# The conditioning product of a two-block transformer kernel: two of its three groups leave block 1

## The chip, the cores and the metric

The kernel runs on one core of a Trainium2 chip. Its time is the device time of one execution in microseconds (us). Three runs of the kernel before gave 1567.90, 1569.79 and 1571.73 us, median 1569.79. TensorE, the matrix engine, is called PE here, VectorE DVE, ScalarE ACT and GpSimd POOL; SP is the engine whose queue issues the loads. [...]

## The reference: what is computed

256 tokens of width 1024 pass through two transformer blocks, all in float32.

Block 1: RMS norm, input projection, a pooling mixer and an attention of 8 heads, output projection with a residual, then a mixture of 32 experts (4 per token), and a final RMS norm. Block 2: a norm, an input projection into 3342 columns, 16 heads of three kinds of attention (6 with a decay, 4 of mLSTM kind, 6 of block kind), an output projection and a gated feed-forward. Block 2 is conditioned on a vector `c`:

```
mod = silu(c) @ w_ada + b_ada                  # 1024 x 6144 weights, 24 MB
sh1, sc1, g1, sh2, sc2, g2 = split(mod, 6)
hn = rms(x, norm1_g) * (1 + sc1) + sh1         # first norm of block 2
x  = x + g1 * (mixer(hn) @ w_out)
hn = rms(x, norm2_g) * (1 + sc2) + sh2         # second norm
x  = x + g2 * ((silu(gate) * up) @ w_down)
```

The product with `w_ada` depends on `c` alone and can be done at any time before its first use. Group 0 of its columns is sh1 and sc1 (used by the first norm of block 2), group 1 is g1 and sh2, group 2 is sc2 and g2 (used only after the attention of block 2).

## The kernel before, in words

All weights come through one ring of 12 slots of 1 MB in SBUF. SP walks a fixed list of chunks (`load(n)`, then a loop over the experts) and, for chunk n, waits until chunk n - 12 has been used (`chunk_used`, counted up by PE). So the order in which PE uses chunks is the order of the list, and a chunk that is moved in PE's program is moved in the list too. An expert takes 12 chunks: 8 of gate and up weights, 4 of down weights.

The conditioning product is 24 chunks, 8 per group. One chunk is `ada(i)` (line 528): four matmuls of 128x512 into the four column strips of PSUM bank 7. A group's eighth chunk is followed by `keep_ada(g)` on DVE (bank 7 plus bias into `mod`), by `turn_mod(g, b)` on PE (four transposes into bank b, line 738) and by `keep_mod(g, b)` on DVE (the turned columns into `modc`). Before: chunks 0 and 1 run at the start, 2 and 3 after the input projection, 4 and 5 ahead of the attention of block 1, 6 to 17 between its heads, 18 to 23 after the output projection.

`attention(block, extra)` is written as a pipeline over heads. In its step i PE does the scores of head i (lines 644 to 649), then what `extra` has for i, then the transposes of the probabilities of head i - 1 (line 670), then the product with the values of head i - 2 (lines 678 to 680). Between the scores and the transposes of a head stand a row maximum on DVE and the exponentials on ACT. Every engine runs its program in order.

After the attention of block 1: two chunks of the output projection on the pooled half (`project_out_start`, line 695) stand beside a chain of norms on DVE that ends in `att_rows`; then transposes of those rows (line 727), the other 6 of 8 parts of the projection, the norm of the rows, their transposes (`turn_rows(4)`), the router, and the loop over the experts. After the experts: sums, the final norm on DVE and ACT, `turn_rows(6)` on PE, and the input projection of block 2 (`project`, line 545).

## Time and profile before

| | |
|---|---|
| runs, median (us) | 1569.79 |
| profiled execution, span from first to last instruction (us) | 1568.5 |
| mean granted PE clock | 0.971 |
| PE busy | 1475.2 us, 94% of the span |
| DVE busy | 324.1 us, 21% |
| ACT busy | 221.4 us, 14% |
| bytes moved, mean rate | 496.98 MB, 317 GB/s |
| chain that ended last | PE 59%, DMA 20%, SP's queue 15%, DVE 3%, issue 2%, ACT 1% |

The profiled execution's span is 1.3 us below the median of the runs. A share of busy time is an average over stages: block 1 ahead of the experts fills about 155 us, the experts 950 us, block 2 460 us. PE's busy time counts occupied time at either clock, so it does not tell a slow stretch from a fast one; PEclk does.

### The profile page before, as it was taken

Reading aid. Unit: us, or ns where it says so; the run is one execution under the profiler, and the core shown is the slowest. Engines: PE = TensorE matmul, PEld = TensorE weight load, DVE = VectorE, ACT = ScalarE, POOL = GpSimd, SP = SyncE. Lnnn points to the kernel's source line nnn. Section 1 sums busy time; section 2 is a strip of 40 time slices with the busy share of each in tenths; the row PEclk is TensorE's granted clock in tenths of the full one; section 3 lists DMA queues with packets and bytes.
Section 4 is the critical chain, followed back from the end, with each engine's and each line's share of the span. In section 5 each row is a group of like instructions: output and inputs, shape, how many; then the busy total and the mean of one; then the engine's idle time right before and its main releaser. Section 6 shows DMA issues by size and latency. Waiting matters only on the chain.

```text
span 1568.5 us, 18813 instructions
## 1 busy us (share of the span) xinstructions
PE 1475.2 (94%) x7278; PEld 787.3 (50%) x7278; DVE 324.1 (21%) x861; ACT 221.4 (14%) x405; POOL 21.8 (1%) x14
## 2 busy tenths in 40 slices
PE   7999999999999999999999999999699998999998
PEld 5655443343343343343333334334499664888843
DVE  5535321121111121121111111112312533000001
ACT  1321011011111011011011111101212430000100
POOL 3100000000000000000000000000000000000000
PEclk9998999999999999999999999999799968999999
DMA  9996999999999999999999999999944103444400
GB/s 331 351 407 264 357 419 417 416 419 419 415 418 419 416 418 418 418 417 418 419 416 419 418 416 418 419 417 414 295 156 156 54 1 107 135 152 143 134 0 27
DMA packets 127123, 496.98 MB, mean 317 GB/s; under 512 B 9825, under 2 KB 51506, under 8 KB 91026
## 3 DMA queue, kind: packets, MB, share of 16 engines
q1 hardware_dynamic: 126484, 495.47, 79.9%
q10 hardware_dynamic: 606, 1.06, 0.2%
q8 instruction: 22, 0.36, 0.1%
q14 instruction: 11, 0.09, 0.0%
HBM read 495.44 MB, written 1.05 MB: 317 GB/s over the span
## 4 chain that ended last, share of the span: by engine, by line
PE 59%; DMA 20%; SPq 15%; DVE 3%; issue 2%; ACT 1%; DVEq 0%; ACTq 0%
DMA ring<-in_w_gate_up_dram 19%; PE PS L989 10%; SPq L459 9%; PE PS L803 9%; PE PS L545 8%; PE PS L828 8%; SPq L462 5%; PE PS L789 5%; PE PS L1005 5%; PE PS L695 3%; PE PS L836 3%; PE PS L644 2%; PE PS L528 1%; ACT work L1155 1%; PE PS L670 1%
## 5 line engine op out<-in xcount | busy, mean ns | idle before, releaser
L803 PE MATMUL PS<-ring,work 128*64 128x512 f32 x2048 | 461.4, 597 | 25.5 <-DMA ring<-in_w_gate_up_dram 25.5
L803 PEld LDWEIGHTS PS<-ring,work 128*64 128x64 f32 x2048 | 138.0, 137 | 331.1 <-issue 232.2
L828 PE MATMUL PS<-ring,work 128*64 128x512 f32 x1024 | 225.1, 592 | 0.0
L1624 DVE TENSOR_SCALAR work<-PS 128x512 f32<-128x512 f32 x32 | 22.1, 691 | 679.9 <-PE PS L803 679.9
L989 PE MATMUL PS<-ring,cols 128*128 128x256 f32 x704 | 156.0, 383 | 2.1 <-issue 2.1
L989 PEld LDWEIGHTS PS<-ring,cols 128*128 128x128 f32 x704 | 134.7, 192 | 20.8 <-DVE cols L1331 2.5
L828 PEld LDWEIGHTS PS<-ring,work 128*64 128x64 f32 x1024 | 71.7, 137 | 132.0 <-issue 129.6
L545 PE MATMUL PS<-ring,cols 128*128 128x240 f32 (+3 forms) x576 | 121.8, 374 | 4.1 <-DVE cols L1331 2.1
L789 PE MATMUL PS<-work,rows 128*128 128x64 f32 x1056 | 125.0, 278 | 0.0
L789 PEld LDWEIGHTS PS<-work,rows 128*128 128x128 f32 x1056 | 123.8, 196 | 0.8 <-DVE work L1601 0.8
L545 PEld LDWEIGHTS PS<-ring,cols 128*128 128x128 f32 x576 | 110.4, 196 | 13.4 <-DVE cols L1331 2.5
L1152 ACT ACTIVATE work<-work 128x512 f32<-128x512 f32 x32 | 20.1, 630 | 469.2 <-DVE work L1624 469.2
L1005 PE MATMUL PS<-ring,work 128*128 128x512 f32 x176 | 75.8, 593 | 0.7 <-ACT work L1282 0.7
L836 PE MATMUL PS<-work 64*128 64x512 f32 x264 | 65.6, 615 | 0.7 <-ACT work L1158 0.7
L695 PE MATMUL PS<-ring,cols 128*128 128x512 f32 x128 | 55.6, 593 | 0.8 <-DVE cols L1333 0.8
L1005 PEld LDWEIGHTS PS<-ring,work 128*128 128x128 f32 x176 | 33.4, 190 | 42.6 <-issue 41.6
L1158 ACT COPY work<-PS 128x512 f32<-128x512 f32 x32 | 18.7, 585 | 236.1 <-PE PS L828 236.1
L836 PEld LDWEIGHTS PS<-work 64*128 64x128 f32 x264 | 22.7, 186 | 43.1 <-issue 41.5
L1619 DVE TENSOR_TENSOR work<-PS,vcol 128x512 f32<-128x512 f32 x33 | 22.8, 691 | 99.2 <-PE PS L789 99.2
L1152 ACT ACT_TABLE_LOAD x32 | 41.1, 1283 | 0.6
L695 PEld LDWEIGHTS PS<-ring,cols 128*128 128x128 f32 x128 | 24.1, 190 | 30.8 <-issue 29.2
L1829 DVE TENSOR_TENSOR rows<-work,PS 128x512 f32<-128x512 f32 x11 | 7.6, 688 | 152.8 <-PE PS L989 152.8
(261 smaller groups left out, 859.6 us busy)
## 6 DMA issues: line engine op xcount, KB each, us to landing
ring<-in_w_gate_up_dram SPq DMA_DIRECT2D x278, 1024.0 KB, 20.4
ring<-in_w_down_dram SPq DMA_DIRECT2D x139, 1024.0 KB, 22.2
ring<-in_w_ada_dram SPq DMA_DIRECT2D x24, 1024.0 KB, 15.9
ring<-in_w_in_dram SPq DMA_DIRECT2D x13, 960.0 KB, 10.8
ring<-in_w_out_dram SPq DMA_DIRECT2D x8, 1024.0 KB, 10.9
ring<-in_w_in_dram SPq DMA_DIRECT2D x3, 1024.0 KB, 12.8
x_sb<-in_x_dram SPq DMA_DIRECT2D x2, 512.0 KB, 3.8
work<-in_band_dram SPq DMA_DIRECT2D x1, 1024.0 KB, 14.9
```

The source lines that it names most:

```text
L459: sp.dma_start(ring[:, s, :], gu_dram[bass.ds(e * KD + c, 1), :, :] .rearrange("o p n -> (o p) n")).then_inc(landed[s], 16)
L462: sp.dma_start(ring[:, s, :].rearrange("p (o k n) -> p o k n", o=1, k=2), dn_dram[bass.ds(e * 4 + (c - KD), 1), :, :, :] .rearrange("o p k ...
L545: mm = pe.matmul(bank(b)[:, t * w:(t + 1) * w], cols[:, k, t * P:(t + 1) * P], chunk(n)[:, k, :], start=(k == 0), stop=(k == KD - 1))
L644: pe.matmul(s[:, a:a + w], q[:, t * P:(t + 1) * P], k[:, 0:w], start=True, stop=ml)
L695: mm = pe.matmul(bank(2 * t + h), cols[:, k, t * P:(t + 1) * P], chunk(base_n + c)[:, k % 2, h * 512:(h + 1) * 512], start=(k == 0), stop= ...
L789: mm = pe.matmul(bank(2)[:, k * CAP:(k + 1) * CAP], rows[:, t, k * P:(k + 1) * P], sel_g[:, t, :], start=(t == 0), stop=(t == NT - 1))
L803: mm = pe.matmul(bank(b)[CAP * h:CAP * (h + 1), :], xg[:, k, :], w[:, b * FE + h * 512:b * FE + (h + 1) * 512], start=False, stop=(k == KD ...
L828: mm = pe.matmul(bank(3)[CAP * h:CAP * (h + 1), :], lhs, w[:, (f % 2) * D + h * 512:(f % 2) * D + (h + 1) * 512], start=False, stop=(f == 7))
L836: mm = pe.matmul(bank(4 + 2 * t + h), sel_t[CAP * h:CAP * (h + 1), t * P:(t + 1) * P], yb[CAP * h:CAP * (h + 1), :], start=False, stop=False)
L989: mm = pe.matmul(bank(4 + 2 * (j % 2) + up)[:, t * CW:(t + 1) * CW], cols[:, k, t * P:(t + 1) * P], chunk(n)[:, k, :], start=(k == 0), sto ...
L1005: mm = pe.matmul(bank(4 + 2 * t + h), h_t[:, f, t * P:(t + 1) * P], chunk(N_DN2 + f // 2)[:, f % 2, h * 512:(h + 1) * 512], start=(f == 0) ...
L1152: return nc.scalar.activation(sg, g_min, ACT.Sigmoid, scale=ALPHA).then_inc(done, 1)
```

## The change

The list of chunks, PE's program and DVE's program are rewritten so that only chunks 0 to 7 (group 0) are computed in block 1: 0 to 3 where they were, 4 to 7 after the output projection. Group 1 (chunks 8 to 15) runs after the experts, once DVE has read the sums from PSUM (`x_summed`), ahead of `turn_rows(6)`; it is turned after two chunks of block 2's input projection. Group 2 (chunks 16 to 23) runs in the second attention, two chunks after the scores of each of the heads 11 to 14 of 16, and is turned in the middle of the second output projection. The gains of the second norm are computed there too. A few small loads come earlier in the list.

```diff
+N_OUT1 = N_KVB + 1
+N_ADA0 = N_OUT1 + 4
+N_MOE = N_ADA0 + KD - ADA_NEXT
+N_ADA1 = N_MOE + EXPERTS * SLOTS
+N_IN2 = N_ADA1 + KD
+N_ADA2 = N_IN2 + len(IN2_CHUNKS)
+N_OUT2 = N_ADA2 + KD
...
             pe.transpose(bank(6)[:, 0:NVEC], vec[:, :], ident[0:NVEC, 0:NVEC]).then_inc(sig["vec2_turned"], 1)
-            ada(ADA_NEXT)
-            ada(ADA_NEXT + 1)
...
-            attention(1, {0: adas(6, 8), 1: adas(8, 9), 2: [pool_sums] + adas(9, 10), 3: adas(10, 12), 4: adas(12, 14),
-                          5: adas(14, 16), 6: adas(16, 17), 7: adas(17, ADA_MID)})
+            attention(1, {2: [pool_sums]})
...
-            for i in range(ADA_MID, ADA_MID + 3):
+            for i in (ADA_NEXT, ADA_NEXT + 1):
                 ada(i)
-            turn_mod(0, 6)
-            turn_mod(1, 5)
-            ada(ADA_MID + 3)
...
             turn_rows(4)
-            ada(ADA_MID + 4)
+            ada(ADA_NEXT + 2)
...
-            ada(ADA_MID + 5)
+            ada(ADA_NEXT + 3)
...
+            pe.wait_ge(sig["x_summed"], 2)
+            for i in range(KD, 2 * KD):
+                ada(i)
             turn_rows(6)
...
-            between = {}
+            between = {2: [lambda: turn_mod(1, 7)]}
...
-            attention(2, started=2)
+            attention(2, {i: adas(2 * KD + 2 * (i - ML_HI - 1), 2 * KD + 2 * (i - ML_HI)) for i in range(ML_HI + 1, ML_HI + 5)},
+                      started=2)
...
             project_out_start(N_OUT2)
+            turn_mod(2, 4)
             project_out_end(N_OUT2)
...
-            attention(1, {0: [lambda: keep_ada(0), square_pooled], 1: [keep_pooled], 3: [keep_pool_sums],
-                          5: [lambda: keep_ada(1)]})
+            attention(1, {0: [square_pooled], 1: [keep_pooled], 3: [keep_pool_sums]})
...
-            keep_mod(0, 6)
-            keep_mod(1, 5)
             keep_cols(lambda k: col("g_ffn_norm", k))
...
             do.step(v.memset(conv_x[:, :, 0:3], 0.0))
+            keep_ada(1)
+            keep_mod(1, 7)
...
+                          ML_HI + 5: [lambda: keep_ada(2)]},
                       started=2)
             keep_cols(lambda k: col("ml_h_g_2", 0) if k == 3 else 1.0)
+            keep_mod(2, 4)
+            norm_gain(1, 32, "norm2_g_2")
```

PE's order in the attention of block 1, one step of the pipeline in the kernel before (L644 and L649 are the scores, L528 two chunks of the conditioning product, L670 the transposes of the head before):

```order
L644 MATMUL PS<-qk 128x128
L649 MATMUL PS<-maskb,identb 128x128
L644 MATMUL PS<-qk 128x256
L649 MATMUL PS<-maskb,identb 128x128
L528 MATMUL PS<-ring,c_rep 32x512 x8
L670 MATMUL PS<-cst,probs 128x128 x3
```

The same step in the changed kernel, whose lines are three further down:

```order
L647 MATMUL PS<-qk 128x128
L652 MATMUL PS<-maskb,identb 128x128
L647 MATMUL PS<-qk 128x256
L652 MATMUL PS<-maskb,identb 128x128
L673 MATMUL PS<-cst,probs 128x128 x3
```

The eight matmuls of two chunks are gone from the step, and with them all 12 chunks from between the heads. PE's order between the experts and block 2 in the changed kernel (L779 closes the sums, L533 is the conditioning product, L506 the transposes of the rows, L550 the input projection of block 2, L740 the turning of group 1):

```order
L779 MATMUL PS<-identb 128x512 x4
L533 MATMUL PS<-ring,c_rep 32x512 x32
L506 MATMUL PS<-cst,rows 128x128 x16
L550 MATMUL PS<-ring,cols 128x240 x32
L740 MATMUL PS<-cst,mod 128x128 x4
L550 MATMUL PS<-ring,cols 128x240 x64
```

In the kernel before, the transposes follow the sums directly; the 32 matmuls of group 1 now stand between them. One of the four late steps of the second attention in the changed kernel:

```order
L647 MATMUL PS<-qk 128x256
L650 MATMUL PS<-work,rowb 128x256
L652 MATMUL PS<-maskb,identb 128x128
L533 MATMUL PS<-ring,c_rep 32x512 x8
L673 MATMUL PS<-cst,probs 128x128 x3
```

In the kernel before, nothing stands there between L649 and L670.

## Rows read from the trace of the kernel before

**Rows 1.** Chain of waits, two experts late in the loop: start, length, what.

```profile
1003.22 24.97 DMA ring<-in_w_gate_up_dram
...
1063.41 24.97 DMA ring<-in_w_gate_up_dram
```

**Rows 2.** Windows, as block 1 hands over to the experts.

```profile
154.00:158.00 4.00, 3.81 (x12) 1.53 (x14) 3.83 (x7) 0.00 (x0) 0.00 (x0) 0.50 0.00 0
```

**Rows 3.** Timeline of PE, attention of block 1: start, length, instruction, idle before.

```profile
68.72 0.49 PE L644 MATMUL PS<-qk 96*128 96x128 f32 x2 [1.66 <-DVE qk L1421]
...
69.74 3.59 PE L528 MATMUL PS<-ring,c_rep 128*32 128x512 f32 x16
...
76.48 1.90 PE L628 MATMUL PS<-cst,work 128*128 128x1 f32 x16
...
86.96 0.55 PE L670 MATMUL PS<-cst,probs 128*128 128x128 f32 x3
...
87.96 0.44 PE L644 MATMUL PS<-qk 96*128 96x128 f32 x2
...
88.93 1.92 PE L528 MATMUL PS<-ring,c_rep 128*32 128x512 f32 x16
...
98.05 0.55 PE L670 MATMUL PS<-cst,probs 128*128 128x128 f32 x3 [0.16 <-ACT probs L1107]
...
99.94 7.09 PE L695 MATMUL PS<-ring,cols 128*128 128x512 f32 x16
106.98 1.09 PE L727 MATMUL PS<-cst,rows 128*128 128x128 f32 x8
```

**Rows 4.** Timeline, end of the first head's exponentials on ACT.

```profile
73.10 0.19 ACT L1107 ACTIVATION_READ_ACCUMULATOR probs<-PS,nmax 128x1 f32 x1
```

**Rows 5.** Windows in the second attention: length, PE, PEld, DVE, ACT, POOL busy, PEclk, DMA.

```profile
1260.00:1262.00 2.00, 2.00 (x10) 1.66 (x10) 0.82 (x4) 1.33 (x5) 0.00 (x0) 0.50 0.00 0
...
1284.00:1286.00 2.00, 2.00 (x14) 1.70 (x14) 0.13 (x1) 0.00 (x0) 0.00 (x0) 0.78 0.00 0
```

**Rows 6.** Timeline, second attention on PE, first at full clock, then at half.

```profile
1232.72 0.48 PE L644 MATMUL PS<-qk 64*128 64x128 f32 x2
...
1235.22 0.48 PE L644 MATMUL PS<-qk 64*128 64x128 f32 x2
...
1256.76 0.79 PE L644 MATMUL PS<-qk 64*128 64x128 f32 x2
...
1259.26 0.85 PE L670 MATMUL PS<-cst,probs 128*128 128x128 f32 x3
...
1261.21 0.79 PE L644 MATMUL PS<-qk 64*128 64x128 f32 x2
...
1279.52 0.90 PE L670 MATMUL PS<-cst,probs 128*128 128x128 f32 x3 [0.43 <-ACT probs L1107]
...
1282.67 2.02 PE L960 MATMUL PS<-mod,cst 128*128 128x512 f32 x2
```

**Rows 7.** Timeline, from the end of the experts to block 2.

```profile
1107.82 2.87 DVE L1687 TENSOR_TENSOR x_sb<-PS,x_sb 128x512 f32<-128x512 f32 x4 [10.91 <-PE PS L781]
...
1119.37 3.67 PE L501 MATMUL PS<-cst,rows 128*128 128x128 f32 x16 [11.16 <-DVE rows L1707]
...
1125.18 5.14 PE L545 MATMUL PS<-ring,cols 128*128 128x240 f32 x12 [2.13 <-DVE cols L1331]
```

**Rows 8.** Windows there.

```profile
1095.00:1100.00 5.00, 4.33 (x29) 2.38 (x30) 0.69 (x1) 0.58 (x1) 0.00 (x0) 1.00 1.06 376
...
1110.00:1115.00 5.00, 0.00 (x0) 0.00 (x0) 4.60 (x12) 3.86 (x8) 0.00 (x0) 0.58 1.08 361
...
1130.00:1135.00 5.00, 5.00 (x23) 4.54 (x23) 0.00 (x0) 0.01 (x1) 0.00 (x0) 0.87 0.02 7
```

**Rows 9.** Timeline after the output projection of block 1.

```profile
131.32 1.09 PE L738 MATMUL PS<-cst,mod 128*128 128x128 f32 x8
...
133.15 0.75 DVE L1320 TENSOR_SCALAR rows<-x_sb,rs 128x1024 f32<-128x1024 f32 x1
```

More of the change, by code:

```diff
@@ L94 @@
 PAIRS = D_FF // CW
-ADA_FIRST, ADA_NEXT, ADA_MID = 2, 4, 18
+ADA_FIRST, ADA_NEXT = 2, 4
 N_IN1 = ADA_FIRST
@@ L100 @@
 N_KVB = N_QB + 1
-N_OUT1 = N_KVB + 1 + ADA_MID - ADA_NEXT
-N_MOE = N_OUT1 + 4 + len(ADA_CHUNKS) - ADA_MID
-N_IN2 = N_MOE + EXPERTS * SLOTS
-N_OUT2 = N_IN2 + len(IN2_CHUNKS)
+N_OUT1 = N_KVB + 1
[5 more added lines that the diff above has]
+N_OUT2 = N_ADA2 + KD
 N_GU2 = N_OUT2 + 4
@@ L116, in ada_at @@
         return N_QB - ADA_NEXT + i
-    return N_KVB + 1 + i - ADA_NEXT if i < ADA_MID else N_OUT1 + 4 + i - ADA_MID
+    if i < KD:
+        return N_ADA0 + i - ADA_NEXT
+    return N_ADA1 + i - KD if i < 2 * KD else N_ADA2 + i - 2 * KD
 ADA_OF = {ada_at(i): gk for i, gk in enumerate(ADA_CHUNKS)}
@@ L448, in _ @@
                     load_small(brouter[:, :], ins["b_router"][0].partition_broadcast(P), "brouter_in")
-                if n == N_OUT1:
+                if n == SLOTS + 4:
                     load_small(gfin[:, :], ins["g_final"].partition_broadcast(P), "gfin_in")
@@ L468, in _ @@
             with sp.If(n_over > 0):
-                sp.wait_ge(chunk_used, N_IN2)
+                sp.wait_ge(chunk_used, N_ADA1)
                 with sp.Fori(0, OVER) as j:
@@ L482, in _ @@
                         sp.sem_inc(sig["o_ring_back"], 1)
-            for n in range(N_IN2, N_END):
+            for n in range(N_ADA1, N_END):
                 load(n)
@@ L758, in _ @@
             mm.then_inc(sig["parts_done"], 1)
-            ada(ADA_MID + 5)
+            ada(ADA_NEXT + 3)
             pe.wait_ge(sig["parts_kept"], 1)
-            pe.wait_ge(sig["mod_cols"], 2)
             for t in range(NT):
@@ L838, in moe_scatter @@
                 mm.then_inc(done, 1)
-            turn_mod(2, 3)
+            turn_mod(0, 3)
             add_zero(4, 6, 7, start=True, stop=False)
@@ L1577, in _ @@
             do.tell(v.tensor_copy(small[:, 4:6], small[:, 0:2]), "shifted")
-            keep_ada(2)
+            keep_ada(0)
             dve.wait_ge(sig["exp_ready"], 2)
@@ L1634, in _ @@
             keep_x(sig["xg_ready"])
-            keep_mod(2, 3)
+            keep_mod(0, 3)
             norm_gain(0, 8, "norm1_g_2")
-            norm_gain(1, 32, "norm2_g_2")
             do.step(v.tensor_tensor_scan(out=upto, data0=ones[0:1, 0:96], data1=flag, initial=0.0,
@@ L1803, in ml_gate @@
                                                in1=rows[:, :, 384:640], op0=ALU.add, op1=ALU.mult), "rows_ready")
-            attention(2, {3: [lambda: conv_silus(0, 1)], 4: [lambda: conv_silus(2, 3)], ML_HI + 2: [ml_squares], ML_HI + 3: [lambda: rstd(S_ML, HD)], ML_HI + 4: [ml_gate]},
+            attention(2, {3: [lambda: conv_silus(0, 1)], 4: [lambda: conv_silus(2, 3)], ML_HI + 2: [ml_squares], ML_HI + 3: [lambda: rstd(S_ML, HD)], ML_HI + 4: [ml_gate],
+                          ML_HI + 5: [lambda: keep_ada(2)]},
                       started=2)
             keep_cols(lambda k: col("ml_h_g_2", 0) if k == 3 else 1.0)
+            keep_mod(2, 4)
+            norm_gain(1, 32, "norm2_g_2")
             def add_gated(base, t, tell, product, last_chunk):
```

## The prediction, made before the changed kernel was run

> **What bounds the kernel now.** I read the chain of waits first, then the windows table by stage, then PE's timeline where the change touches it. In the expert loop the chain runs through the loads of the ring: one long piece of DMA comes every 60.19 us (1003.22 to 1063.41), which is two experts, 30.1 us each or 2.51 us per chunk of 1 MB [rows 1]. So the experts, most of the time, are bound by the rate of the loads, and their end follows from the moment at which their stream starts. What sets that moment? Ahead of the first expert the DMA stands still, 0 GB/s from 154 to 158 us [rows 2]: all 12 slots are full and SP waits for PE to use one. Block 1 ahead of the experts is therefore bound by PE and by what PE waits for, and a us won or lost there moves the whole loop by a us. Block 2 is a chain of norms, projections and attention steps in which PE is the bound or waits for DVE and ACT.
>
> **What is removed ahead of the experts.** Two chunks stood ahead of the first scores. They end before those scores, which wait 1.66 us more for DVE's copies [rows 3]; taking them out gives nothing. Twelve stood between the heads. A pair takes 1.92 us at full clock and 3.59 us at half [rows 3]. A late step is scores 88.93 - 87.96 = 0.97, pair 1.92, transposes and values 87.96 - 86.96 = 1.00 us, in all 3.9. With PE alone a step without the pair would be 1.97 us, and the chain through DVE and ACT would hold it near 2.3.
>
> But the clock decides this term. Between the k-head transposes and the first scores PE now has 1.66 us idle plus the 1.9 us that the pair filled, and after two heads of scores it waits again: the first exponentials are done at 73.10 + 0.19 = 73.29 [rows 4], since an activation table is loaded ahead of them. In the kernel before, the clock was already at half after the first of these gaps: the pair at 69.74 takes 3.59 us instead of 1.92, and after it the full clock is back [rows 3]. The changed kernel has the longer gap and not the pair, the one dense piece of work there. Do the heads alone bring the clock back? The second attention is the nearest row. Its late heads run at half clock: 4.45 us per head (1256.76 to 1261.21), against 2.50 (1232.72 to 1235.22) in its early heads [rows 6]. From 1260 to 1262 PE is busy for 2.00 of 2.00 us and the granted clock is 0.50; it returns only in the window 1284 to 1286, when the wide matmul of 1282.67 (L960) has run [rows 5, 6]. Heads alone did not lift it. I take half clock for the whole first attention.
>
> At half clock transposes and values take 1261.21 - 1259.26 = 1.95 us, 1.95 times the 1.00 at full [rows 3, 6]; the scores by the same factor 1.9. A step is 3.85 us (bounds: 1.97, PE alone at full clock, and 4.45, the step of the second attention, which has bias matmuls more). That is what a step with a pair cost at full clock. The attention then goes: to 74.0 for the first transposes, a third step of 1.9 + 3.7 (the pool sums, 1.90 at full) + 1.95 = 7.5, five steps of 3.85 = 19.2, and a tail of 0.3 wait and 3.15 (1279.52 to 1282.67 in the second attention; 98.05 to 99.94, 1.89, at full). It ends at 104.1, where it ended at 99.94 [rows 3]: **+4.2 us**. Two things make it worse than even: the steps with one chunk or none get slower, and the tail is at half.
>
> The chunks of the output projection at 99.94 take 7.09 us, and the transposes behind them start at 106.98, just when PE is free [rows 3]: there is no slack, so a slower PE costs in full. The clock has to come back inside them. After the pair it took 3.6 us of dense work [rows 3], after 1125.18 some 6.1 us (full clock again at about 1131.3, from 0.87 over the window 1130 to 1135) [rows 7, 8]; half of that is lost, 1.8 to 3.0 us. I take **+2.0**, with 0 as the other end.
>
> After the projection two chunks remain where four and two turnings stood. They lay beside DVE's norm of the second row tile, whose last step runs 133.15 to 133.90; turning both groups was 1.02 us (131.32 to 132.34) [rows 9]. The transposes of that tile follow this step and gain at most 0.4 us. PE now idles some 2.4 us there, after which the clock may fall sooner than before, costing up to 2. Together **+0.3** (-0.4 to +2.0). Waits on DVE that go (`keep_ada`, `keep_mod`) are under 0.7 us each and stood beside PE. The small loads that move up in SP's queue are not waited for, and the ring is full ahead of the experts as before.
>
> **Group 1 in the final norm.** PE idled for 11.16 us ahead of the transposes at 1119.37 [rows 7]. DVE has read the sums at 1107.82 + 2.87 = 1110.69. Eight chunks are four pairs, 7.7 us at full clock, 14.4 at half; the clock is 0.58 over 1110 to 1115, so at half from about 1110.8 [rows 8]. With 3.6 to 6 us of dense work to bring it back, they end at 1120 to 1121.5. The transposes may then start up to 1.5 us later than at 1119.37, but at full clock they take 2 us (8 of them 1.09) rather than 3.67 [rows 3, 7]. The input projection starts about where it did, 1125.18, and no longer spends 6.1 us at half. Gain 3.0, at most 4; if the clock falls again behind the transposes, 1. **-3.0.** The data: the mixed rate of 376 GB/s over 1095 to 1100, between 418 (a chunk in 2.51 us) and 361, puts the last expert's chunk at about 1096.5 [rows 1, 8]. The eighth chunk then lands at 1096.5 + 8 x 2.51 = 1116.6, in time for the eighth product, and those of the projection behind it. Turning group 1 inside the projection adds **+0.5** (half of 1.02 [rows 9]); behind DVE's wait for it nothing is due for several us.
>
> **Group 2 in the second attention.** The first pair comes at half clock, +3.6. It is just what lifted the clock at 69.74, so the next three steps are 2.50 + 1.92 = 4.42 rather than 4.45, -0.1. Behind them the last head and the tail run at full clock: its scores and the step before, about -1.6, and 1.89 - 3.15 = -1.3 [rows 3, 6]. Together **+0.6** (-0.5 to +4, if only the second or third pair lifts it). Turning group 2 in the output projection is another **+0.5**, with DVE's read of it done before its sums are due.
>
> [...]
>
> **Sum.** 4.2 + 2.0 + 0.3 - 3.0 + 0.5 + 0.6 + 0.5 = +5.1 us on a span of 1568.5, so 1573.6; the median of the runs lies 1.3 above that span, so about 1575 us.
>
> **Rivals.** First, the first attention runs at full clock. To 74.0 as above; then 3.9 for the third step, 5 x 2.3 and a tail of 3.2 end it at 92.6, which is -7.3; the output projection loses nothing. -7.3 + 0.3 - 3.0 + 0.5 + 0.6 + 0.5 = -8.4, about 1561.5. For it: these heads use 96 rows of the array where the second attention's use 64 [rows 3, 6], and have no narrow bias matmuls, so they are denser; early heads of the second attention held the full clock. Against: they did not win it back. A chance of 0.17. If the clock returns halfway through, the terms cancel: the attention about -1.5, in all -2.6 to +2: 1567 to 1572, chance 0.15.
>
> Second, the loads: 16 chunks fewer ahead of the experts are 16 x 2.51 = 40 us of stream. Had the DMA been the bound there, the time would be near 1535. The standing DMA at 154 to 158 [rows 2] is against it: 0.02; with small surprises of the same sign (a shorter stretch at half clock after the router) I give 0.04 more.
>
> Third, the pairs in the second attention do not lift the clock. Then all four cost 3.6 = 14.4 instead of 0.6, in all +18.9, 1589. It decides from the point at which the first pair ends: if the step behind it is still 4.45. The pair at 69.74 is against it: 0.04. My forecast, with its own range 1572 to 1580, keeps 0.58.
>
> Slower by over 0.2% (about 3 us, what a measurement of this kernel can tell from no change) is 0.58 + 0.04 = 0.62; within it 0.15; faster 0.17 + 0.06 = 0.23. The range 1562 to 1581 takes in the first rival and the halfway case and leaves the third out.
>
> **What would show it.** In the changed profile: PEclk 0.50 from about 70 us through the first attention; a step of about 3.85 us there; the chunks at L697 starting near 104 and taking 8 to 10 us; the first expert about 6 us later than 155; group 1's matmuls from 1117 or so on, first slow, then 0.96 per chunk, and the input projection at 1.00 from the start; the clock at 1.00 from head 12 of the second attention on. The forecast is wrong if PEclk is 1.00 in the first attention and its steps take 2.3 us, or if the expert loop's length differs from the one before.

## The result, and the profile after

The changed kernel takes 1572.36 us (median of 20 runs, 1568.23 to 1575.84), the kernel before 1568.89 us in the same session (20 runs, 1564.78 to 1571.73). The ratio is 1.0022, with a 95% interval of 1.0014 to 1.0031: 3.5 us slower. The prediction was 1575 us, slower the likeliest. The profiled execution of the changed kernel has a span of 1571.0 us, the one of before 1568.5; the stages below therefore explain 2.5 us of difference, from one execution of each.

Where did the time go? I read the start of each stage from PE's timeline in both profiles; the end is the profile's span. The kernels e1 to e12 are the experiments described further down, and the same stages are used for all of them. Profiles with the same program up to the first scores start these anywhere from 65.4 to 70.7 us, so a stage is read as a difference within its row. In us:

| kernel | scores 1 | out. proj. 1 | first expert | last expert | input proj. 2 | scores 2 | out. proj. 2 | gated product | end |
|---|---|---|---|---|---|---|---|---|---|
| before | 68.7 | 99.9 | 154.2 | 1074.3 | 1125.2 | 1217.0 | 1288.3 | 1327.9 | 1568.5 |
| after | 68.7 | 103.0 | 157.9 | 1075.6 | 1126.2 | 1217.1 | 1290.1 | 1330.2 | 1571.0 |
| e1 pair back | 67.9 | 99.1 | 156.9 | 1075.8 | 1126.5 | 1217.4 | 1288.5 | 1328.6 | 1568.4 |
| e2 two dense | 68.9 | 92.4 | 147.1 | 1067.3 | 1117.0 | 1207.9 | 1278.9 | 1319.0 | 1558.8 |
| e3 without both | 68.5 | 102.1 | 158.5 | 1077.0 | 1128.0 | 1218.9 | 1290.6 | 1330.7 | 1571.7 |
| e4 without group 2 | 66.1 | 100.5 | 156.9 | 1075.5 | 1125.7 | 1216.7 | 1288.6 | 1328.7 | 1569.8 |
| e5 warm heads | 70.7 | 104.3 | 160.7 | 1078.9 | 1129.2 | 1220.2 | 1289.6 | 1329.7 | 1570.5 |
| e6 before, warm | 68.8 | 100.0 | 154.2 | 1074.4 | 1125.3 | 1215.5 | 1278.4 | 1318.1 | 1558.6 |
| e7 both | 66.5 | 98.0 | 153.3 | 1073.2 | 1122.8 | 1213.7 | 1282.8 | 1322.9 | 1563.5 |
| e8 and tail | 65.9 | 89.4 | 143.4 | 1062.3 | 1113.0 | 1202.3 | 1271.7 | 1311.7 | 1552.5 |
| e9 guard | 65.4 | 90.1 | 143.3 | 1062.5 | 1113.0 | 1202.3 | 1271.4 | 1311.4 | 1552.1 |
| e10 before, heads, tail | 70.5 | 100.0 | 150.3 | 1068.2 | 1119.1 | 1210.7 | 1273.6 | 1313.3 | 1554.5 |
| e11 all | 67.4 | 92.1 | 144.7 | 1060.4 | 1111.9 | 1202.8 | 1272.4 | 1311.8 | 1550.0 |
| e12 all, sums last | 69.0 | 93.7 | 146.3 | 1064.4 | 1116.3 | 1205.6 | 1274.7 | 1314.1 | 1552.3 |

The first attention of the changed kernel, PE's timeline and a window of it (length, PE, PEld, DVE, ACT, POOL busy, PEclk, DMA share, GB/s), answers to [rows 3]. PEclk is the clock granted to PE as a share of the full one. In steps of 0.25 us over 68 to 76 us of the kernel before it is 1.00 or 0.50, and 0.95 and 0.73 in the two steps in which it changes; 1.00 is called full here, 0.50 half.

```profile
68.74 0.58 PE L647 MATMUL PS<-qk 96*128 96x128 f32 x2 [3.51 <-DVE qk L1424]
...
76.34 3.52 PE L631 MATMUL PS<-cst,work 128*128 128x1 f32 x16
...
85.09 0.74 PE L647 MATMUL PS<-qk 96*128 96x128 f32 x2
...
88.61 0.74 PE L647 MATMUL PS<-qk 96*128 96x128 f32 x2
...
102.96 8.88 PE L697 MATMUL PS<-ring,cols 128*128 128x512 f32 x16
111.67 0.49 PE L729 MATMUL PS<-cst,rows 128*128 128x128 f32 x3
```

```profile
70.00:98.00 28.00, 26.16 (x112) 22.67 (x111) 9.28 (x29) 11.32 (x35) 0.00 (x0) 0.50 0.39 164
154.00:158.00 4.00, 3.66 (x18) 3.07 (x19) 0.92 (x3) 0.00 (x0) 0.00 (x0) 0.50 0.00 0
```

The clock is 0.50 from the first scores on, and PE is busy 26 of 28 us. A step is 88.61 - 85.09 = 3.52 us, and has no product of a chunk in it; before, it cost 3.9 us with a pair. So twelve chunks left the heads and the attention got 3.0 us longer (its end is at 102.96 against 99.94). All 20 runs of the changed kernel have a mean granted clock of 0.969 to 0.974. The DMA still stands at 154 to 158 us, as in [rows 2]; SP's queue has a single wait of 17.2 us there for PE's use of a chunk (L801), 18.5 us before (L803).

PE waits 1.84 us for the first exponentials, ahead of which ACT has a table load of 1.28 us, in the kernel before (first line) as in the changed one:

```profile
70.94 1.28 ACT L1107 ACT_TABLE_LOAD   x1 [7.29 <-DVE nmax L1451]
```

```profile
71.64 1.28 ACT L1110 ACT_TABLE_LOAD   x1 [8.58 <-DVE nmax L1454]
...
74.04 0.90 PE L673 MATMUL PS<-cst,probs 128*128 128x128 f32 x3 [1.84 <-ACT probs L1110]
```

Group 1 ahead of the final norm's transposes, PE's timeline, answers to [rows 7]; and the chain of waits (start, length, what), answers to [rows 1]:

```profile
1106.63 1.99 PE L834 MATMUL PS<-work 64*128 64x512 f32 x8 [0.69 <-ACT work L1161]
...
1112.11 5.36 PE L533 MATMUL PS<-ring,c_rep 128*32 128x512 f32 x48 [2.52 <-DVE x_sb L1686]
1118.40 1.06 PE L533 MATMUL PS<-ring,c_rep 128*32 128x512 f32 x8 [0.94 <-DMA ring<-in_w_ada_dram]
1120.91 1.06 PE L533 MATMUL PS<-ring,c_rep 128*32 128x512 f32 x8 [1.44 <-DMA ring<-in_w_ada_dram]
1121.90 1.97 PE L506 MATMUL PS<-cst,rows 128*128 128x128 f32 x16
1126.21 5.97 PE L550 MATMUL PS<-ring,cols 128*128 128x240 f32 x20 [2.34 <-ACT cols L1048]
```

```profile
1065.15 24.60 DMA ring<-in_w_gate_up_dram
...
1094.44 26.42 DMA ring<-in_w_ada_dram
```

```profile
1127.00:1130.00 3.00, 3.00 (x10) 2.55 (x9) 0.00 (x0) 0.00 (x0) 0.00 (x0) 0.52 1.12 366
1131.00:1135.00 4.00, 4.00 (x21) 3.75 (x20) 0.00 (x0) 0.29 (x1) 0.00 (x0) 1.00 1.09 363
```

Six chunks run at full clock at once (1.00 in every window from 1110 to 1126 us; in the kernel before, with PE idle there, it fell at about 1110.8 [rows 8]). The last two wait for their loads: the chain no longer passes through DVE here, as it did before, but through the load that is issued at 1094.44 and lands at 1120.9. The transposes take 1.97 us instead of 3.67, and the projection starts 1.0 us later than before. In it the clock is at half once more, around 1127 to 1130.

Group 2 in the second attention, PE's timeline and windows, answers to [rows 5, 6]:

```profile
1259.98 3.64 PE L533 MATMUL PS<-ring,c_rep 128*32 128x512 f32 x16
...
1264.68 0.48 PE L647 MATMUL PS<-qk 64*128 64x128 f32 x2
...
1269.16 0.49 PE L647 MATMUL PS<-qk 64*128 64x128 f32 x2
...
1281.97 0.55 PE L673 MATMUL PS<-cst,probs 128*128 128x128 f32 x3 [1.30 <-ACT probs L1110]
...
1283.87 1.74 PE L962 MATMUL PS<-mod,cst 128*128 128x512 f32 x2
1285.41 2.97 PE L506 MATMUL PS<-cst,rows 128*128 128x128 f32 x16
```

```profile
1260.00:1262.00 2.00, 2.00 (x13) 0.58 (x16) 1.22 (x5) 0.77 (x3) 0.00 (x0) 0.50 0.00 0
...
1264.00:1280.00 16.00, 16.00 (x120) 8.71 (x118) 9.63 (x35) 5.83 (x18) 0.00 (x0) 1.00 1.09 354
1284.00:1287.00 3.00, 3.00 (x11) 1.78 (x11) 1.11 (x2) 0.00 (x0) 0.00 (x0) 0.53 1.09 346
```

The first pair runs at half, and behind it the clock is at full; the steps there take 4.48 us with a pair. The tail then waits 1.30 us for ACT, and at about 1284.1 the clock falls again, in the wide matmul of 1283.87 (L962). The transposes behind it take 2.97 us, against 2.11 in the kernel before.

### The profile page after: what moved, and what is told of

Same layout as the page of the kernel before. It is cut to its first block, busy times and chain, and to the rows that moved or that the text cites. A ratio compares the mean times of both kernels' runs of the same rounds, so it can differ in the third digit from the quotient of the medians.

```text
span 1571.0 us, 18812 instructions
## 1 busy us (share of the span) xinstructions
PE 1477.1 (94%) x7278; PEld 792.1 (50%) x7278; DVE 324.8 (21%) x861; ACT 221.6 (14%) x405; POOL 21.9 (1%) x14
## 4 chain that ended last, share of the span: by engine, by line
PE 59%; DMA 21%; SPq 12%; DVE 3%; issue 2%; ACT 2%; DVEq 0%; ACTq 0%
DMA ring<-in_w_gate_up_dram 19%; PE PS L801 10%; PE PS L992 10%; PE PS L550 8%; SPq L464 8%; PE PS L826 7%; PE PS L1008 5%; PE PS L787 5%; SPq L467 4%; PE PS L697 3%; PE PS L834 2%; PE PS L647 2%; DMA ring<-in_w_ada_dram 2%; PE PS L533 1%; ACT work L1158 1%
## 5 line engine op out<-in xcount | busy, mean ns | idle before, releaser
L801 PE MATMUL PS<-ring,work 128*64 128x512 f32 x2048 | 460.1, 597 | 24.3 <-DMA ring<-in_w_gate_up_dram 24.3
L801 PEld LDWEIGHTS PS<-ring,work 128*64 128x64 f32 x2048 | 139.6, 137 | 327.0 <-issue 233.2
L550 PE MATMUL PS<-ring,cols 128*128 128x240 f32 (+3 forms) x576 | 120.6, 371 | 4.3 <-ACT cols L1048 2.3
L550 PEld LDWEIGHTS PS<-ring,cols 128*128 128x128 f32 x576 | 109.4, 194 | 13.1 <-DVE cols L1334 2.5
L697 PEld LDWEIGHTS PS<-ring,cols 128*128 128x128 f32 x128 | 24.7, 196 | 31.5 <-issue 29.8
## 6 DMA issues: line engine op xcount, KB each, us to landing
ring<-in_w_ada_dram SPq DMA_DIRECT2D x24, 1024.0 KB, 11.1
ring<-in_w_in_dram SPq DMA_DIRECT2D x13, 960.0 KB, 10.8
```

The lines of the kernel that those rows point to most:

```text
L550: mm = pe.matmul(bank(b)[:, t * w:(t + 1) * w], cols[:, k, t * P:(t + 1) * P], chunk(n)[:, k, :], start=(k == 0), stop=(k == KD - 1))
L697: mm = pe.matmul(bank(2 * t + h), cols[:, k, t * P:(t + 1) * P], chunk(base_n + c)[:, k % 2, h * 512:(h + 1) * 512], start=(k == 0), stop= ...
L801: mm = pe.matmul(bank(b)[CAP * h:CAP * (h + 1), :], xg[:, k, :], w[:, b * FE + h * 512:b * FE + (h + 1) * 512], start=False, stop=(k == KD ...
```

## Experiments

Every ratio is that of the kernel's runs to those of the kernel before, with its 95% interval, from five rounds.

**e1: four chunks back in block 1.** To the changed kernel:

```diff
-N_OUT1 = N_KVB + 1
-N_ADA0 = N_OUT1 + 4
-N_MOE = N_ADA0 + KD - ADA_NEXT
+N_ADA0 = N_KVB + 1
+N_OUT1 = N_ADA0 + KD - ADA_NEXT
+N_MOE = N_OUT1 + 4
...
+            ada(ADA_NEXT)
+            ada(ADA_NEXT + 1)
...
-            attention(1, {2: [pool_sums]})
+            attention(1, {0: adas(6, 8), 2: [pool_sums]})
```

> The changed kernel with chunks 4 to 7 of the first group back where the kernel before has them: the products of 4 and 5 ahead of attention 1's first scores, of 6 and 7 between heads 0 and 1, their loads ahead of the output projection's weights. Groups 1 and 2 stay where the change put them. Theory A (four chunks' dense products warm the clock, after which the heads keep it): the clock returns near 73 us as before the change, heads without chunks then take 2.3 to 2.6 us instead of 3.52 to 3.85, attention 1 ends at 91 to 95 us instead of 103.0, the whole kernel is 8 to 11 us faster than the changed one and 5 to 8 faster than the one before. Theory B (the heads alone lose the clock at once, whatever came ahead): the clock is at half again by head 1 or 2, attention 1 ends at 102 to 107 us, the whole is within 2 us of the changed kernel. Theory C (the start of the stream is late, so that time gained in attention 1 is lost to loads behind it): attention 1 ends at 91 to 95 us but the expert loop's last down product is within 1 us of the changed kernel's, and the total gains under 2 us.

Measured: 1570.49 us (1561.58 to 1573.18, 12 runs), 1.0013 (0.9997 to 1.0029). PE's timeline and windows:

```profile
74.66 1.95 PE L633 MATMUL PS<-cst,work 128*128 128x1 f32 x16
...
79.33 0.90 PE L675 MATMUL PS<-cst,probs 128*128 128x128 f32 x3 [0.26 <-ACT probs L1108]
...
99.07 9.05 PE L699 MATMUL PS<-ring,cols 128*128 128x512 f32 x16
```

```profile
74.00:78.00 4.00, 3.81 (x30) 3.16 (x29) 3.65 (x11) 1.50 (x5) 0.00 (x0) 1.00 1.01 422
78.00:82.00 4.00, 3.74 (x21) 3.30 (x21) 1.19 (x5) 3.00 (x10) 0.00 (x0) 0.64 1.02 426
82.00:92.00 10.00, 10.00 (x44) 8.78 (x44) 2.66 (x9) 3.67 (x13) 0.00 (x0) 0.50 1.01 421
```

The pair did bring the clock back (1.00 from 74 to 78), and then it fell again at about 79.1, 2.5 us behind the end of the pool's sums, with PE busy 3.74 of the 4 us from 78 to 82. So theory A holds for the rise and fails for what follows. Theory B has the place wrong, but its total came: by the ratios e1 is some 1.4 us below the changed kernel, and the intervals overlap. The attention ends at 99.1, between the two theories. It is also no test of the attention alone. The stage is 3.0 us shorter than in the changed kernel (31.2 against 34.2), and the way from the output projection to the first expert is 2.9 us longer (57.8 against 54.9): the four products are missing there, and from 134 us on the clock is at 0.50. One run of the 12 stands apart, 1561.6 us at a mean clock of 0.978, where the other eleven have 0.970 to 0.973; it was not traced.

**e2: two dense products added.** Nothing is taken away; eight matmuls into an unused bank, behind the first scores:

```diff
+            def warm():
+                pe.wait_ge(sig["vec2_cols"], 1)
+                for _ in range(2):
+                    for j in range(4):
+                        pe.matmul(bank(6)[32 * j:32 * j + 32, :], c_rep[:, 0, :], x_sb[:, 0, 0:512],
+                                  start=True, stop=True)
-            attention(1, {2: [pool_sums]})
+            attention(1, {0: [warm], 2: [pool_sums]})
```

> The changed kernel with work added and none removed: two products of the shape of a chunk's (four 128 by 32 matmuls over 512 columns each, 8 in all, 3.64 us at half clock and 1.90 at full by the changed kernel's rows) into an unused PSUM bank behind the first scores of attention 1. Theory A (the clock's level is what attention 1 pays for): if two chunks are enough to bring the clock back, about 73 to 77 us, attention 1 gets shorter in spite of the added work, ends at 93 to 98 us instead of 103.0, and the total falls by 5 to 9 us against the changed kernel. Theory B (added work is only added): attention 1 ends 2 to 4 us later, at 105 to 107, the total rises by 2 to 4 us. If the two chunks are too few to move the clock, the second holds too, and then the first is open.

Measured: 1560.95 us (1557.81 to 1563.45, 7 runs), 0.9967 (0.9953 to 0.9980). PE's timeline and a window:

```profile
70.19 3.23 PE L640 MATMUL PS<-x_sb,c_rep 128*32 128x512 f32 x16
...
92.42 7.08 PE L705 MATMUL PS<-ring,cols 128*128 128x512 f32 x16
```

```profile
82.00:92.00 10.00, 9.12 (x64) 7.10 (x63) 3.45 (x12) 6.48 (x21) 0.00 (x0) 1.00 0.21 88
```

Against 1.0022 for the changed kernel, 3 us of work added make it 0.55%, some 8.6 us, faster. The mean clocks of its seven runs are 0.979 to 0.983, all above those of the changed kernel. The attention ends at 92.42 instead of 102.96 (10.5 us), the first expert starts 10.8 us earlier, the last one 8.4. It is the cleanest test of the prediction's main term: what the first attention pays for is the clock, and the first rival's time (1561.5, its end of attention 92.6) is what the kernel takes when the clock is held.

**e3 and e4: groups left out.** e3 leaves out both groups' loads and products, e4 those of group 2:

```diff
-            for i in range(KD, 2 * KD):
-                ada(i)
...
-            attention(2, {i: adas(2 * KD + 2 * (i - ML_HI - 1), 2 * KD + 2 * (i - ML_HI)) for i in range(ML_HI + 1, ML_HI + 5)},
-                      started=2)
+            attention(2, started=2)
```

> The changed kernel with groups 1 and 2 of the conditioning product left out: their 16 loads and 64 matmuls are not issued, the two additions on VectorE read the sum's own bias instead of the product. All else is the changed kernel's. It says what both groups cost in their new places. By my terms for the changed kernel (12.0 us of products ahead of the first row of the final norm against a wait of 9 that was there anyway, and 10 us of them between heads that they bring back to full clock) it should be 1 to 6 us faster than the changed kernel: the final norm starts when the last expert's rows are added, at half clock, and attention 2 ends as in the kernel before. Rival (the products' warmth is worth more than their time): equal or up to 3 us slower than the changed kernel. Rival (the stream's 8 MB of loads is what they cost): 6 to 15 us faster.

> The changed kernel with group 2 alone left out (8 loads, 32 matmuls between the last heads of attention 2; the addition on VectorE reads the bias instead). Against the changed kernel it is group 2's price, against the kernel without both it is group 1's. Mine for group 2: attention 2 at half clock throughout takes 4.45 us a head as before the change, the spread of the turned vectors starts within 0.5 us of where it starts in the kernel before relative to the heads' start, so that the total is 0.5 to 3 us below the changed kernel. For group 1: the final norm's work keeps its 1.00 clock, so that this kernel is 0 to 3 us slower than the kernel without both. Rival for group 2: the pairs' clock gives back more than the pairs cost, and it is 1 to 3 us slower without them.

Measured: e3 1573.05 us (1571.56 to 1575.29), 1.0043 (1.0029 to 1.0058); e4 1572.07 us (1570.93 to 1572.40), 1.0035 (1.0022 to 1.0048). Neither is faster than the changed kernel (1.0022, 1.0014 to 1.0031), with 16 and 8 MB of loads and 64 and 32 matmuls less. My own expectations, 1 to 6 us less for e3 and 0.5 to 3 us less for e4, both missed: by the runs the rival fits better, that the full clock which the products bring ("warmth" in the texts) is worth at least what they take. The intervals of the three overlap, so the sign of each group's worth isn't shown. PE's timeline of e3 at the final norm:

```profile
1122.19 3.65 PE L506 MATMUL PS<-cst,rows 128*128 128x128 f32 x16 [11.26 <-DVE rows L1704]
1127.97 7.38 PE L550 MATMUL PS<-ring,cols 128*128 128x240 f32 x27 [2.13 <-DVE cols L1331]
```

The idle time is back, 11.26 us, and the transposes are at half again. From the last expert to the projection it takes 50.96 us, against 50.57 with group 1 in the changed kernel: eight products at that place cost nothing, in one profile of each. From the second attention's first scores to the output projection e3 takes 71.74, e4 71.92 and the changed kernel 72.94 us, so group 2 costs 1.0 to 1.2 us there.

**e5 and e6: full clock in the second attention.** Four matmuls 128 by 128 in unused columns of a bank, in each of the steps 6 to 10 of the changed kernel (e5) and 6 to 15 of the kernel before (e6, whose edit this is; e5's range ends at `ML_HI + 1`, and group 2's chunks follow):

```diff
+            def warm(i, n):
+                for _ in range(n):
+                    pe.matmul(bank(2 + (HEADS + i - 1) % 2)[:, 384:512], ident, x_sb[:, 0, 0:P], start=True, stop=True)
...
+            attention(2, {i: [lambda i=i: warm(i, 4)] for i in range(ML_LO, ML_HI + MOBA)}, started=2)
```

> The changed kernel with four more 128 by 128 matmuls (shape of the transposes, 0.55 us for three by the rows, so about 0.7 for four at full clock) in each of the five steps 6 to 10 of attention 2, between a head's scores and the transposes of the head before, in unused columns of a PSUM bank. Theory A (the half clock is what the mLSTM heads and the first pairs of group 2 pay): the clock stays at full beyond 1246 us, the heads' steps take 2.9 to 3.3 us instead of 4.45, the first pair 1.9 instead of 3.6, the total falls by 3 to 7 us against the changed kernel. Theory B (the chip wants something other than these matmuls, or the heads' own waits decide): the clock falls at 1246 all the same, each step at half gets 0.9 to 1.3 us longer, the total rises by 2 to 5 us.

> The kernel before the change with the same four added matmuls in steps 6 to 15 of attention 2 (it has no products of chunks there, and ran from 1247.3 to 1284.9 us at half clock). Theory A: full clock to the end of the heads, steps of 2.9 to 3.3 us instead of 4.45, attention 2 is 8 to 14 us shorter, and so is the total; since the change's group 2 takes its time between the same heads, this also says that the warmth, not the product, is what can be had there. Theory B: the clock is at half as before, each of the ten steps gets 1 to 1.3 us longer, the total 8 to 13 us longer.

Measured: e5 1568.63 us (1561.93 to 1572.30, 12 runs), 1.0009 (0.9996 to 1.0021); e6 1557.29 us (1554.29 to 1560.44, 6 runs), 0.9940 (0.9920 to 0.9959). Windows of the same stretch, first of the kernel before, then of e6:

```profile
1247.00:1285.00 38.00, 37.57 (x145) 27.42 (x146) 16.76 (x62) 12.96 (x39) 0.00 (x0) 0.51 0.00 1
```

```profile
1247.00:1285.00 38.00, 36.38 (x226) 26.27 (x226) 17.89 (x63) 15.63 (x45) 0.00 (x0) 1.00 0.01 1
```

PE's timeline of e6:

```profile
1250.16 0.49 PE L649 MATMUL PS<-qk 64*128 64x128 f32 x2
...
1251.60 1.11 PE L635 MATMUL PS<-x_sb,cst 128*128 128x128 f32 x8
...
1253.59 0.48 PE L649 MATMUL PS<-qk 64*128 64x128 f32 x2
```

Forty matmuls were added, a step takes 1253.59 - 1250.16 = 3.43 us instead of 4.45, and the stage from scores to output projection is 71.3 - 62.9 = 8.4 us shorter. Theory A holds. In e5 the same is seen up to the first pair of group 2, which now takes 1.92 us instead of 3.64, and the stage is 3.5 us shorter (69.4 against 72.9). Against the changed kernel's 1.0022 the total of e5 is some 2 us lower, which the intervals don't separate; its profiled execution is the slowest of its 12, and started the first scores 2 us later.

**e7 and e8: both additions, and the tail.** e7 is e2's two dense products and e5's added matmuls together; e8 adds four more dense products in the tail (e8's edit against e7):

```diff
             ada(ADA_NEXT + 3)
+            dense(1)
...
+            dense(3)
             pe.wait_ge(sig["routed"], 1)
```

> The changed kernel with both additions: two products of a chunk's shape behind the first scores of attention 1, and the four added matmuls in steps 6 to 10 of attention 2. If the two are independent, its distance to the changed kernel is the sum of theirs: 9.5 us for the first (1572.4 and the measured 1561, set against the runs of before), 3 to 7 for the second, so 1554 to 1559 us. If the second does nothing (theory B of the other runs), 1562 to 1567.

> As the one with both additions, and four more products of a chunk's shape in the tail of block 1: one behind the router's partial sums, three ahead of the wait for the routing (1.89 us of waiting there), so that the gather of the first expert's rows (7.09 us at half clock for 32 matmuls, 3.5 to 4 at full) is at full clock. Theory A (what the start of the experts gains passes on): first expert 4 to 7 us earlier, total 2 to 6 us below the kernel with both additions. Theory B (the loads bound the experts from the tenth on, at 30.12 us each against 28.37, so an earlier start is spent in waits for loads): first expert 4 to 7 us earlier but the last one within 1.5 us, total within 1.5 us.

Measured: e7 1557.88 us (1553.10 to 1565.36, 6 runs), 0.9940 (0.9920 to 0.9959); e8 1555.80 us (1554.35 to 1559.88, 6 runs), 0.9941 (0.9923 to 0.9959). e7 is in the range that the sum of its two parts gave (1554 to 1559). e7 and e8 are equal up to the tail, yet their profiles are not. The same window, first of e7, then of e8:

```profile
76.00:92.00 16.00, 16.00 (x69) 14.13 (x69) 3.70 (x13) 7.31 (x25) 0.00 (x0) 0.50 0.38 160
```

```profile
76.00:92.00 16.00, 15.10 (x92) 10.75 (x91) 7.02 (x22) 8.67 (x29) 0.00 (x0) 1.00 0.38 159
```

In e7's profiled execution the clock fell at 75.0, as the pool's sums ended, and stayed at half for the rest of the attention; in e8's it held. The one reaches the output projection 31.5 us after its first scores, the other 23.6. The profiled run of e7 is the one at 1565.36 us, with a mean clock of 0.978; its other five lie from 1553.1 to 1559.7, with 0.984 to 0.989. So the same instructions have two outcomes, about 8 us of attention apart, and this is a good part of the spread of e7's runs. The tail's products gained less than I expected: from output projection to first expert 54.0 us in e8 against 54.7 in e2 and 55.3 in e7. The first expert did start 9.9 us earlier than in e7's profile, but 8 of these are the attention's clock. The 4 to 7 us expected of the tail did not come, since the clock fell again as the first gather began, at about 135.9 (6.89 us for 32 matmuls).

**e9 to e12: a guard, the old places, and all together.** e9 is e8 with one dense product behind the pool's sums. e10 is the kernel before with e6's matmuls and three dense products ahead of the wait for the routing. e11 is e9 with products in more waits. In e9 and e11 the product behind the sums writes over them before VectorE reads them, so the scale of the mixer's norm is another there; e12 is e11 with that product ahead of the sums. First e9's edit against e8, then what e11 adds to it:

```diff
-            attention(1, {0: [dense], 2: [pool_sums]})
+            attention(1, {0: [dense], 2: [pool_sums, lambda: dense(1)]})
...
+            dense(2)
             add_zero(4, 6, 7, start=True, stop=False)
...
+            dense(2, 5, mod[:, 1, :])
             pe.wait_ge(sig["gate_used"], 4)
-            turn_rows(9)
+            turn_rows(9, fill=lambda: dense(3, 5, mod[:, 1, :]))
+            dense(2, 5, mod[:, 1, :])
```

> As the one with warm tail, and one more product of a chunk's shape behind the pool's sums in step 2 of attention 1 (16 matmuls of one column, 1.90 us). In the profile of the kernel with both additions the clock fell at 75.0 us, with those sums at 73.11, and in that of the warm tail, equal to it up to there, it did not. Theory (sums of one column are what the clock falls on): full clock from 71 us to the end of attention 1, a narrower spread of the runs, total 1553 to 1558 us. Rival (the fall is by chance and one product more is only 0.95 us more): spread as before, 1557 to 1562 us.

> The kernel before the change with the four added matmuls in steps 6 to 15 of attention 2 and three products of a chunk's shape ahead of the wait for the routing, none else (its attention 1 has the chunks). It sets the old places of the three groups beside the new ones, both with the clock held. Theory A (the change lost only by the clock; at full clock the place of a product is worth what it covers): within 3 us of the changed kernel with its additions, 1553 to 1558 us. Theory B (16 chunks less in block 1 are worth 10 us or more once the clock is held): 1560 to 1566 us. Theory C (the old places were the better ones in any case): 1546 to 1552.

> As the one with the guard, and more products of a chunk's shape in waits of TensorE: two ahead of the zeroing before the first gather, and 2, 3 and 2 around the turning of the normed rows ahead of block 2's gated product (its first 5 us ran at half clock, the waits there are 1.75, 3.27 and 2.13 us). Theory A (half clock in the first gather and in the first gated products is on the path): gather 3.5 us shorter, gated product 4 to 5 us shorter, total 4 to 8 us below the kernel with the guard, 1547 to 1552. Theory B (the gather's gain goes to the loads, the added products outlast the waits): within 2 us of it.

> As the kernel with all additions, with the added product of step 2 of attention 1 ahead of the pool's sums instead of behind them, so that the whole of the reference is computed again (in the two kernels with the guard the added product wrote over the pool's sums before VectorE read them, and the scale of the mixer's norm came out of other numbers). If a product on either side of the sums of one column holds the clock, it is as the kernel with all additions: 1549 to 1557 us, 10 to 17 below the kernel before. If it has to stand behind them, some of the runs lose the clock in attention 1, and the highest is 1562 or more.

Measured: e9 1555.61 us (1552.93 to 1560.18, 6 runs), 0.9923 (0.9904 to 0.9942); e10 1555.73 us (1551.46 to 1559.98, 6 runs), 0.9919 (0.9899 to 0.9939); e11 1555.67 us (1548.96 to 1560.13, 6 runs), 0.9918 (0.9895 to 0.9942); e12 1563.66 us (1551.04 to 1564.91, 12 runs), 0.9962 (0.9943 to 0.9982).

With the guard behind the sums none of 12 runs (e9, e11) is above 1560.2 us. With it ahead of them, 7 of 12 lie from 1563.4 to 1564.9 and 5 from 1551.0 to 1560.8; e12's expectation had named just this, a highest run of 1562 or more, as the sign that the product has to stand behind them. The mean clocks go with it, 0.983 to 0.986 in the seven and 0.987 to 0.993 in the five. These are the two outcomes of e7 again, I think, but the profiled execution of e12 is one of the five (1.00 from 74 to 92 us), and none of the seven was traced.

That the sums, sixteen matmuls of one column, lose the clock rests on place (e7 as they end, at 75.0; e1 2.5 us behind their end) and on this spread. Against it stand the kernels with no product at either side of the sums: none of e8's 6 runs is above 1559.9, and one of e7's 6 is. If the sums alone did it, these should look like e12. So the moment at which the dense products come, rather than the sums, is a rival that no run here takes apart, and the mechanism is open.

e10 against e8 and e9 compares the old places of the chunks with the new ones when the heads run at full clock on both sides: no difference that these runs tell (0.9919 against 0.9941 and 0.9923). In the profiles of e8 and e10 two terms stand against each other. From the first scores to the first expert the new places take 77.5 us instead of 79.8, 2.3 us less (e8's first expert is 6.9 us earlier, but 4.6 of these lie ahead of the first scores, where profiles differ by as much without a change). The way from the last expert to the output projection of block 2 is 3.9 us longer (209.3 against 205.4). From the first scores to the end the old places are 2.6 us shorter in these two profiles (1484.0 against 1486.6), which is less than either kernel's runs spread.

In e11 the gather runs at full clock, PE's timeline of e8 and then of e11:

```profile
135.64 6.89 PE L802 MATMUL PS<-work,rows 128*128 128x64 f32 x32 [0.60 <-DVE work L1617]
```

```profile
140.02 3.79 PE L804 MATMUL PS<-work,rows 128*128 128x64 f32 x32
```

From the first expert to the last it takes 915.7 instead of e9's 919.2 us, and from the gated product to the end 238.2 instead of 240.6 to 240.8. Up to the first expert, though, e11 is only 0.6 us shorter than e9 (52.6 us from the output projection instead of 53.2); the added products and waits take the rest back. The medians of e9 and e11 don't differ, which is theory B's total. Of the kernels that compute the whole reference e10, e6, e7 and e8 are the fastest (0.9919 to 0.9941 of the kernel before, their intervals overlap), so the old places with 40 added matmuls are as good as anything here.

## Why the prediction was right

The kernel became slower, and the main term came as forecast. The sum was +5.1 us, where the profiles have +2.5 and the medians +3.5. That it came this near is in part luck: it is too high by 5.2 us over four terms and too low by 2.6 over the others. Its steps against the profiles, in us of shift that each stage adds (from the stage starts):

| step | predicted | measured |
|---|---|---|
| first attention | +4.2 | +3.0 |
| output projection 1, first part (111.67 against 106.98) | +2.0 | +1.7 |
| tail of block 1 | +0.3 | -1.0 |
| expert loop | 0 | -2.4 |
| group 1, final norm, input projection | -2.5 | -1.2 |
| group 2 in the second attention | +0.6 | +1.6 |
| turning group 2 | +0.5 | +0.45 |
| the rest | 0 | +0.3 |
| sum | +5.1 | +2.5 |

**The clock in the first attention: right.** It is at 0.50 throughout. e2 shows by one addition that this is the cause, and what it is worth, 10.5 us of attention. The size was 1.2 us too large. The factor of 1.95 set a half-clock row of the second attention (1.95 us) against a full-clock row of the first (1.00), whose heads are not the same. At half clock the first attention takes 1.70 us for the scores and 1.82 for transposes and values, so five steps were taken at 3.85 where they measured 3.52; the tail was 0.3 us longer than taken.

**The output projection: right.** No slack there, the second part starts 1.7 us later still.

**The tail of block 1: wrong in sign.** The clock stayed up there until 147.5 instead of 141.4, and PE gained 1.0 us rather than losing 0.3.

**"A us won or lost there moves the whole loop by a us": right for large shifts, wrong for this one.** Between e8 and e5 the first expert starts 17.3 us apart (143.4, 160.7), the last one 16.5 (1062.3, 1078.9). For the change itself 3.7 became 1.3, and a loop of another length is one of the signs that the prediction named against itself. It is the largest error in the sum. Of the 2.4 us lost between, 0.5 is the first expert (30.0 against 30.5, less of it at half clock). The loads' pace of 30.12 per expert sets in one expert later after the change (behind the first expert nine follow at 28.37, against eight), which is another 1.8. Half of the loss is there by 196 us: SP issues its first load of the loop 3.2 us later than before (162.04 against 158.82), and by 196 us the changed kernel has moved 1.0 MB less, by my estimate 2.4 us at the loop's 418 GB/s. Where the rest goes, and why the pace set in later, I could not settle; the length of the loop varies from 915.7 to 920.2 us over these kernels.

**Group 1: the place right, two steps wrong that cancel in part.** The products run in the wait for the norm, and the transposes behind them at full clock. The prediction had the clock fall ahead of the products and come back inside them; it stayed at 1.00. And it had the eighth chunk landing at 1116.6, from a guess at the mixed rate in [rows 8]; it landed at 1120.9 (1119.5 with the loop's shift of 1.3 us taken off), and so the last two products waited 0.94 and 1.44 us for loads. They ended at 1122.0, which less the shift is 1120.7, inside the 1120 to 1121.5 of the forecast, by other steps than it names. Then the clock fell again behind the transposes, at about 1127, for which the prediction had set the gain at 1 instead of 3. The whole measured a gain of 1.2 with the turning, against 2.5.

**Group 2: right to 1 us.** The first pair lifted the clock, the steps cost 4.48 as against 4.42 predicted. What was missed lies in the tail: 1.30 us waiting for ACT and a clock that fell again at 1284.1. Against heads at half clock the pairs are nearly free (e4, 1.0 us), against heads held at full clock they are not: e10 needs 62.9 us for the stage without them, with twenty more added matmuls, and e8 69.4 with them.

**The rivals.** The first one's time was 1561.5, and e2 gives 1561 with its condition, full clock, made true; its step of 2.3 us was an estimate for which no row was named, and e2 has one of 87.23 - 85.00 = 2.23 us, from scores to scores (L655). So the forecast rested on one binary question, which the rows of the second attention answered rightly; e7 and e8 show that the same heads can also go the other way. The whole range, 1562 to 1581, reached down to the first rival's time, so that the measured time lies inside it says little by itself. The loads (second rival) and the pairs without effect (third) did not come. Two sums of the rivals do not come out: the halfway case gives -2.6 to -0.6 us by the terms named, not up to +2, and 40 us off the time before is 1530, not 1535. Neither changes the forecast.

PE busy without a gap did not bring the full clock back here: it is busy 10.00 of 10.00 us at 0.50 in e1 (82 to 92 us) and 16.00 of 16.00 in e7 (76 to 92 us).

Transposes are part of every head here, and the products and plain matmuls that lifted or held the clock are not transposes. Transposes themselves are seen at either clock: the sixteen of the final norm take 1.97 us at 1.00 in the changed kernel and 3.67 at 0.50 in the one before. Whether they help to keep the heads at half, no run here took apart.

## What to carry to other kernels

Before dense work is taken out of a stretch of thin matmuls (attention heads, transposes, sums of one column), ask what the clock does without it. Here the first attention got 3.0 us longer with twelve chunks less, at 0.50 throughout, and 10.5 us shorter again with two products added. Read PEclk beside PE's busy time. Where PE is busy and the clock at half, a few added products of a chunk's shape are a cheap test, in e2 worth 8.6 us against 3 us of work. And when runs of one program spread widely (0.9% in e12, 0.4% in the kernel before), compare their clocks before anything else.

## What the runs showed of the hardware that I had not expected

- The same heads ran at either level for 16 us and more. PE was busy 16.00 of 16.00 us at 0.50 in e7 and 15.10 of 16.00 at 1.00 in e8, with the same instructions; 26.16 us busy of 28 in the changed kernel (70 to 98 us, 0.50) did not lift it.
- By times and mean clocks, which level it was differed between kernels that differ in the place of one product near the start of the stretch, and between runs of one kernel. With one dense product (1.07 us) ahead of the pool's sums 7 of 12 runs are in the group from 1563.4 us on, with it behind them none of 12, and without it one of 12 (e7 and e8). What tips it is open.
- Forty added matmuls of 128 by 128 made a stage 8.4 us shorter, with the clock at 1.00 instead of 0.51 from 1247 to 1285 us (e6). They are plain products with the identity; the heads already have transposes of that size.
- One chunk's load took 26.42 us from issue to landing behind the expert loop (1094.44 to 1120.86 in the changed kernel), against a median of 11.1 us for the 24 loads of its kind. The DMA moved 413 GB/s in that time, by my estimate some ten chunks of 1 MB, and the last product of group 1 waited for it, with PE idle for 1.44 us.
